# Mixing and routing the next block of tokens between the expert operations

## The reference, cut to what matters

```
g    = gelu(y_s5);  s5 = rmsnorm(g * sigmoid(g @ w_glu))      # w_glu 1024 x 1024
m2   = rmsnorm of (y * silu(z)), by halves of 512
x    = x + concat(s5, m2) @ w_out                             # w_out 2048 x 1024
h    = rmsnorm(x);  q = h @ w_q                               # w_q 1024 x 2048: 8 heads x 2 halves x 128
s    = q . sub_keys                                           # 16 key rows of 128 scores per token
top 16 of each key row -> 16 x 16 sums per head -> top 16 of those: 8 x 16 = 128 experts, gate = softmax
x    = x + sum over 128 experts of gate * gelu(u[e] . h) * v[e]
y    = rmsnorm(x)
```

## Time and profile before

| what | us |
|---|---|
| median of 3 runs | 4684.44 (4682.33 to 4685.42) |
| the profiled execution's own time | 4684.25 |
| its span in the profile | 4682.5 |
| first transfer of `mix_out` | 1352.42 |
| first transfer of `route_and_experts` | 1792.81 |
| first gather | 1891.59 |

### The profile page before, as it was taken

How to read it: one execution, slowest core, us unless ns; L and a number is a source line. 1 busy time by engine, 2 the same in 40 slices (tenths; PEclk the granted TensorE clock), 3 DMA queues, 4 the chain that set the end, 5 groups by cost and what they waited for, 6 DMA issues and landing times.

```text
span 4682.5 us, 54327 instructions
## 1 busy us (share of the span) xinstructions
PE 2876.1 (61%) x17688; PEld 1481.5 (32%) x17688; DVE 2462.9 (53%) x4924; ACT 1290.2 (28%) x3117; POOL 1411.9 (30%) x1547
## 2 busy tenths in 40 slices
PE   8999590745559995554654744645645546447444
PEld 5766460723334444221311411411312213114110
DVE  1000529248831113576576675674675765766754
ACT  1110020112222321333333333333333333333332
POOL 3000320301100000444444444444443444444443
PEclk9999755866779997665755755756757658658555
DMA  4111300121131112899999999999999999999998
GB/s 163 52 50 36 75 2 2 43 101 30 39 160 66 46 54 97 349 421 420 415 421 400 421 421 405 420 420 404 420 419 400 421 419 405 421 407 420 421 415 362
DMA packets 258478, 1271.27 MB, mean 271 GB/s; under 512 B 63984, under 2 KB 98672, under 8 KB 118128
## 3 DMA queue, kind: packets, MB, share of 16 engines
q0 software_dynamic: 156672, 1140.92, 58.8%
q1 hardware_dynamic: 101536, 127.12, 8.2%
HBM read 1225.69 MB, written 40.09 MB: 270 GB/s over the span
## 4 chain that ended last, share of the span: by engine, by line
DMA 40%; issue 7%; PE 6%; ACT 4%; DVE 4%; POOL 1%; POOLq 0%; SPq 0%; DVEq 0%; ACTq 0%
DMA pe_ring<-in_uv,pe_index_now 39%; PE pe_acc L1858 3%; DVE pe_ring L1781 2%; PE pe_ps_q L1831 2%; ACT pe_mark L1629 1%; ACT pe_weight L1631 1%; PE pe_ps_t L1851 1%; ACT L1629 1%; DVE pe_work_a L1662 1%; POOL pe_ring L1570 1%; ACT L1620 1%; DMA pe_w_q<-in_w_q 0%; DVE pe_pos L1714 0%; DVE pe_work_b L1715 0%; PE pe_ps_s L1841 0%
## 5 line engine op out<-in xcount | busy, mean ns | idle before, releaser
L1781 DVE CUSTOM_DVE_ANT_0 pe_ring<-pe_ring,pe_h_rep 128x1024 f32<-128x1024 f32 x1088 | 1330.7, 1226 | 961.3 <-DMA pe_ring<-in_uv,pe_index_now 881.3
L1858 PE MATMUL pe_acc<-pe_ring,pe_weight 128*32 128x256 f32 x8704 | 1018.5, 560 | 1232.3 <-ACT pe_weight L1631 1203.4
L1570 POOL DMA_INDIRECT pe_ring<-in_uv,pe_index_now x1088 | 1198.0, 1101 | 1471.2 <-PE pe_acc L1858 1275.3
L1858 PEld LDWEIGHTS pe_acc<-pe_ring,pe_weight 128*32 128x32 f32 x8704 | 210.8, 131 | 1973.1 <-ACT pe_weight L1631 1863.6
L1629 ACT ACTIVATE pe_mark<-pe_eye,pe_dot 128x32 f32<-128x32 f32 x1088 | 349.4, 321 | 1744.1 <-DVE pe_dot L1781 1690.3
L1631 ACT ACTIVATE pe_weight<-pe_mark,pe_gate_now 128x32 f32<-128x32 f32 x1088 | 349.5, 321 | 35.1
L1831 PE MATMUL pe_ps_q<-pe_h_t,pe_w_q 128*128 128x128 f32 x2304 | 329.5, 303 | 1.9 <-DMA pe_w_q<-in_w_q 1.9
L1831 PEld LDWEIGHTS pe_ps_q<-pe_h_t,pe_w_q 128*128 128x128 f32 x2304 | 302.7, 213 | 60.1 <-issue 57.8
L372 PE MATMUL pj_bank<-pj_w_in,pj_normed_t 128*128 128x512 f32 (+1 forms) x720 | 267.6, 529 | 5.7 <-DMA pj_w_in<-in_w_in 5.7
L1392 PE MATMUL mo_ps_out<-mo_w_out,mo_both_t 128*128 128x512 f32 x576 | 251.1, 594 | 14.8 <-DVE mo_both_t L1342 11.9
L378 PE MATMUL pj_bank<-pj_normed_t,pj_w_in 128*128 128x128 f32 x1728 | 195.2, 275 | 0.0
(11 more groups left out here) (312 smaller groups left out, 3222.6 us busy)
## 6 DMA issues: line engine op xcount, KB each, us to landing
pe_ring<-in_uv,pe_index_now POOLq DMA_INDIRECT x1088
pe_w_q<-in_w_q SPq DMA_DIRECT2D x4, 2048.0 KB, 18.3
m2s_window<-scratch_xbc SPq DMA_DIRECT2D x8, 786.0 KB
pj_w_in<-in_w_in SPq DMA_DIRECT2D x1, 6144.0 KB, 39.5
scratch_xbc<-pj_chan_out SPq DMA_DIRECT2D x8, 768.0 KB, 5.1
pj_x<-in_x_all SPq DMA_DIRECT2D x9, 512.0 KB
scratch_u<-pj_token_out SPq DMA_DIRECT2D x9, 512.0 KB, 2.6
scratch_z<-pj_token_out SPq DMA_DIRECT2D x9, 512.0 KB, 3.7
```

The lines of the kernel that those rows point to most:

```text
L1570: nc.gpsimd.indirect_dma_start(out=ring[:, p, :], out_offset=None, in_=D["uv"], in_offset=bass.IndirectOffsetOnAxis(ap=row, axis=0)).then_ ...
L1781: V.tensor_tensor_reduce(out=ring[:, p, 0:D_MODEL], in0=ring[:, p, 0:D_MODEL], in1=h_rep[:, g % 2, :], scale=1.0, scalar=0.0, op0=ALU.mult ...
L1858: last = T.matmul(acc[j * PER:(j + 1) * PER, g % 2, 0:COLS], lhs(j), src[:, j * COLS:(j + 1) * COLS], start=first, stop=final)
```

## The change

`mix_out` is emptied, and its work becomes part of the last stage. The nine tiles are cut into four blocks, (0), (1, 2), (3, 4, 5), (6, 7, 8). For each block, mixing and routing are done for all its tiles together: matmuls of up to 384 columns with the weights as the standing operand. The weights are no longer held: for each block `w_glu`, `w_out` and `w_q` are loaded again in 20 pieces of 128 x 8 x 256 (rows of 1 KB, 1 MB in all) through three buffers `w_buf`. Block 0 is done ahead of the gathers; each other block is done between the expert operations of the block before it, by a list of steps with places, `after[n]`, that every engine's list follows. The router's selection is done in four units of four key rows and two heads, for all tiles of the block. All loops are written out. The ring has six slots in place of eight. POOL no longer copies the indices; ACT no longer copies x, h and gate (x is loaded a second time and h made again, on DVE).

The core of the diff:

```
-    RING = 8
-    OPS = SLOTS
+    RING = 6
+    WB = 3
...
+    BLOCK_OF = ((0,), (1, 2), (3, 4, 5), (6, 7, 8))
...
+    UNITS, UNIT = 4, 4
+    PIECES = 4 + 8 + PH
+    GLU, OUT, QUERY = 0, 4, 12
+
+    def block_steps(nb):
...
+        for i in range(nb):
+            t = 8 * i
+            add(t, "sp_y", i)
+            add(t, "sp_x0", i)
+            for dt, name in ((2, "act_g"), (3, "dve_gate"), (3, "pe_g"), (4, "act_gt"), (4, "act_sq"), (5, "dve_mn"), (6, "pe_m"), (7, "dve_mt")):
+                add(t + dt, name, i)
+        g0 = 8 * (nb - 1) + 6
+        done = {}
+        for c in range(KT):
+            for dt, name in ((0, "pe_glu"), (1, "act_sig"), (2, "dve_s5"), (3, "act_ss"), (4, "pe_ss")):
+                add(g0 + 2 * c + dt, name, c)
...
+        for q in range(4):
+            for half in range(2):
+                for i in range(nb):
+                    add(o0 + (2 * q + half) * nb + i, "pe_o", q, half, i)
...
+        for j in range(PAIR):
+            for dt, name in ((0, "pe_q"), (1, "act_q"), (2, "pe_s"), (3, "act_s")):
+                add(q0 + 3 * j + dt, name, j)
...
+        for u in range(UNITS):
+            k0 = q0 + 12 * u + 13
+            for n in range(16):
+                add(k0 + n, "dve_k", u, n)
+            add(k0 + 12, "act_e", u)
+        for s in range(PIECES):
+            add(0 if s < WB else done[s - WB], "sp_w", s)
...
+        s, room = FIRST[b - 1] * SLOTS, len(BLOCK_OF[b - 1]) * SLOTS - 26
+        split = int(0.42 * room)
+        for t, name, args in ev:
+            n = s + (t * split // q0 if t < q0 else split + (t - q0) * (room - split) // (last - q0))
+            after[n].append((name, (b,) + args))
...
+            def weights(b, s):
+                W = PIECES * b + s
+                if W >= WB:
+                    b0, s0 = divmod(W - WB, PIECES)
+                    if s0 < OUT:
+                        sp.wait_ge(glu_made, KT * b0 + 2 * s0 + 2)
...
+                sp.dma_start(w_buf[:, W % WB], rows).then_inc(w_in[W % WB], 16)
...
+                if n >= RING:
+                    pool.wait_ge(op_done, n - RING + 1)
+                    settle(pool, settled)
```

More of the change, by code:

```diff
@@ new lines, in route_and_experts @@
+    opening = []
+    after = [[] for n in range(NT)]
+    for b, tiles in enumerate(BLOCK_OF):
+        ev, q0, last = block_steps(len(tiles))
+        if b == 0:
+            opening += [(name, (b,) + args) for t, name, args in ev]
+            continue
+        s, room = FIRST[b - 1] * SLOTS, len(BLOCK_OF[b - 1]) * SLOTS - 26
[3 more added lines that the diff above has]
+            after[n].append((name, (b,) + args))
@@ L1445, in route_and_experts @@
+    uses = [(name, args) for steps in [opening] + after for name, args in steps if name in ("pe_g", "pe_m", "pe_h", "pe_c", "pe_rep")]
+    TURN = {use: n for n, use in enumerate(uses)}
     with ExitStack() as ctx:
@@ new lines, in _ @@
+            act.wait_ge(eps_set, 1)
+            for name, args in opening:
+                step(name, args)
+            for n in range(NT):
+                k, s = divmod(n, SLOTS)
+                p = n % RING
+                if s == 0:
+                    act.wait_ge(index_ready, k + 1)
+                act.wait_ge(dots_ready, n + 1)
+                A(mark[:, p, :], eye[:], ACT.Gelu_apprx_tanh, scale=dot[:, p:p + 1]).then_inc(mark_ready, 1)
+                act.wait_ge(mark_ready, n + 1)
+                A(weight[:, p, :], mark[:, p, :], ACT.Copy, scale=choice[:, k % 2, 1, s:s + 1]).then_inc(weight_ready, 1)
+                for name, args in after[n]:
+                    step(name, args)
@@ L1800, in _ @@
             V.tensor_copy(same[:], eye[:].unsqueeze(1).to_broadcast([P, GROUPS, PER])).then_inc(made, 1)
-            chain.start(0)
-            for g in range(ROUTE_STEPS):
-                route(0, g, False)
-            with dve.Fori(0, MAIN_TILES) as k:
-                tile(k, GROUPS, True)
-            tile(MAIN_TILES, SAMPLE // PER, False)
+            for name, args in opening:
+                step(name, args)
+            for n in range(NT):
+                G, p = n // PER, n % RING
+                if n % PER == 0:
+                    dve.wait_ge(taken, TURN["pe_rep", (G,)] + 1)
+                dve.wait_ge(rows_in[p], 16 * (n // RING + 1))
+                V.tensor_tensor_reduce(out=ring[:, p, 0:D_MODEL], in0=ring[:, p, 0:D_MODEL], in1=h_rep[:, G % 2, :],
+                                       scale=1.0, scalar=0.0, op0=ALU.mult, op1=ALU.add, accum_out=dot[:, p:p + 1]).then_inc(dots_ready, 1)
+                for name, args in after[n]:
+                    step(name, args)
         @block.tensor
@@ L1848, in repeat, with turn @@
[L1848 to L1855 removed]
+            def turn(use, src):
+                u = TURN[use]
+                if u:
+                    pe.wait_ge(taken, u)
+                for c in range(KT):
+                    last = T.transpose(ps_t[:, c, :], src[:, c * P:(c + 1) * P], ident[:])
+                last.then_inc(turned, 1)
```

1035 lines of the change are left out of this document (516 added, 519 removed).

## The result

The changed kernel takes 4722.96 us (median of 4 runs, 4720.95 to 4730.76), the kernel before 4684.22 beside it: a ratio of 1.0086, interval 1.0071 to 1.0101. It is slower by 0.86%, where 4650 and "faster" was forecast; the time lies within the range of 4560 to 4775, and on the other side of the kernel before. The profiled execution is the longest of the four, 4730.76 us.

The account below looks back on a forecast made before the run. It took the last stage as bound by the gathers' bytes, the earlier ones by PE and a one-tile chain. Opening 1529, DMA 2952, key selection 91, chains 60 and ends 16 gave 4648, stated as 4650; range 4560 to 4775.

Parts of the forecast that it names:

- first gather: Opening with block 0's work: the first gather goes out at about 1529 us instead of 1891.59, a gain of 362.
- 1088 gathers: Gather stage: every gather of 128 rows x 8 KB takes 2.485 us, 2704 us in all.
- pieces, loads, stores: DMA added within the gathers: 60 reloaded weight pieces 186 us, inputs, x and x_mid 62 us.
- key selection on DVE: Key steps within the gathers: DVE binds, adding 59 us in block 1, 32 in block 2, none in block 3; 91.
- chains through PE and ACT: Gated and output steps within the gathers: 11 us chains not all hidden by the ring, 20 us a block, 60 together.
- the 66 us at the loop ends: Eight loop ends of the old gather stage, where DVE waits for instructions: about 66 us lost, which unrolling removes.
- bound of 140: Upper end for the chain cost: 140 us if each of 24 gated steps loses the 5.8 us beyond the ring's margin.
- sign for "wrong": Gather stage: the prediction is wrong if DMA stays under 0.9 outside the key steps of blocks 1 and 2.
- weights late or chains longer: Slower outcome within the gathers, from late weight pieces or longer PE and ACT chains; chance 0.33.
- Weights late: Output products of blocks 1 to 3: pieces taking 23 us make PE wait and DMA idle; 4758 us, chance 0.33.
- POOL's starving: Key steps of blocks 1 and 2: DVE's denser work holds up POOL's gather issue; 5120 us, chance 0.02.
- all hidden: Gather stage: no chain cost of 60 us and weight pieces at 2.5 us each; 4554 us, chance 0.1.

Follow-up runs that it names:

- gathers alone: The changed kernel without mixing, routing and weights of blocks 1 to 3, all tiles using tile 0's experts and inputs: 4287.02 us, ratio 0.9149 to the kernel before.
- transfers alone: The changed kernel with blocks 1 to 3 reduced to their transfers beside the gathers, nothing computing on what they bring: 4510.46 us, ratio 0.9627 to the kernel before.
- no keys: The changed kernel without DVE's key selection for blocks 1 to 3, all tiles using tile 0's experts and gates: 4618.70 us, ratio 0.9859 to the kernel before.

## Why the prediction was wrong

The idea held: 367 us are gained ahead of the gathers (1891.6 to 1524.6; 362 forecast), and the work returns within them, but at some 400 us and not 330. The forecast gain was the small difference of two large sums, 34 us, and two terms were off by more than that, both to the slow side.

| term | forecast | measured | from |
|---|---|---|---|
| first gather | 1529 | 1525 | the trace after |
| 1088 gathers | 2704 | 2748 | gathers alone |
| pieces, loads, stores | 248 | 223 | transfers alone less gathers alone |
| key selection on DVE | 91 | 106 | no keys |
| chains through PE and ACT | 60 | 107 | the rest: 213 - 106 |
| ends | 16 | 14 | what is left of the gathers alone: 4287 - 1525 - 2748 |

The measured column adds to 4723. The fourth and fifth terms are split by leaving out one of them, and parts that overlap may be counted to either; the fifth is a remainder, with no run of its own. The second and third are not cut at quite the same place: the gathers alone load x a second time for every tile, some 10 us in all (an estimate: 8 x 0.52 MB at 420 GB/s), which the forecast has among its 248.

*The gathers' pace (44 us).* The step that failed is "Unrolling takes the 66 us at the loop ends away; my sum has that already, as it starts from 2.485". A gather without loops and beside nothing but its own tile's x and y takes 2.528. The 2.485 is the spacing of two dots with nothing else under way; in the gathers alone it is still the common one (median 2.49), but the mean is 2.528, with DMA busy throughout. The bytes of x and y are some 20 us of the 44 (an estimate: 8.9 MB at 420 GB/s); the rest was not traced to a cause. And most of the 66 was never lost at the loop ends. Before, the dots stop there for 11.4 us from start to start, and the next ones follow after some 1.15 each from the full ring. From the last dot of tile 0's loop to the sixth after it:

```profile
2219.60 1.23 DVE L1781 CUSTOM_DVE_ANT_0 pe_ring<-pe_ring,pe_h_rep 128x1024 f32<-128x1024 f32 x1 [1.26 <-DMA pe_ring<-in_uv,pe_index_now]
...
2237.85 1.23 DVE L1781 CUSTOM_DVE_ANT_0 pe_ring<-pe_ring,pe_h_rep 128x1024 f32<-128x1024 f32 x1 [1.02 <-DMA pe_ring<-in_uv,pe_index_now]
```

These six spacings take 18.3 us where six of 2.484 take 14.9: 3.4 lost, and about as much at each of seven ends (0.3 at the eighth). From the first dot to the last the gathers took 2775 us before and take 2748 alone without loops, so 27 of the 66 were gained; the other part was the pace itself, and the trace of the kernel before already held it.

*The chains (47 us).* "I take 20 for each block": without the keys' share, tile 0's stretch loses 96 - 40 = 56, that of tiles 1 and 2 80 - 42 = 38, that of tiles 3 to 5 only 5. I spread one price evenly, though block 1 has 42 gathers for its mixing and block 3 has 150. My line on the gated step names the gathers that should pass in it for blocks 2 and 3 (2.5 and 3.9) and leaves out block 1, where by the same list only 1.4 do: 3.5 us of transfers for steps that follow each other after 7.2. The bound of 140 that I named was the better guide for a short stretch: there the chain isn't a loss on top of DMA, it is the pace, and the transfers under it are free (72 us given back by leaving out 186 us of pieces).

*The keys.* 106 for 91, but 40, 42 and 32 by blocks, not 59, 32 and 0. The forecast compared sums of busy time with sums of transfer time; lumps of more than the ring's margin cost time where the sums say hidden. Where I had DVE bind it did: it is busy for 156.9 of 165.4 us in block 1's key steps (1774.60 to 1940.00).

*The signs and the rivals.* The sign for "wrong" came as named: DMA stands at 0.84 over block 1's first 42 gathers, where no key step lies. The 0.33 was for "weights late or chains longer", and the second half came, for which no rival had a price. "Weights late" was on the right side, for the wrong reason: pieces are slow to land (medians of 18 to 43 us), but SP runs far enough ahead. PE waits for a piece 10.6 us in the whole run:

```profile
PE pe_bg L1879 <- DMA pe_w_buf<-in_w_out: 10.6, 3, 9.4
```

(total us, times, longest). With two buffers and 1 KB rows a part of that rival does appear (43.7 us). The rule of the Trainium skill, "DMA: Bandwidth & Descriptors", section Queues, rings and completion order, that each engine goes round its queue rows packet by packet, and by which alone 23 us a piece would hold, is borne out in so far as 23 lies among the medians of 17.7, 26.6 and 42.8; it says nothing of who waits for the pieces. Neither POOL's starving (an issue takes 1.13 us on the mean beside the steps, 0.97 in the last 320 gathers) nor "all hidden" occurred.

## What to carry to other kernels

Work moved under a bound resource cost, at each place of this kernel, about the longest of transfers, busiest engine and the chain through all of them (the chain in block 1's mixing, the transfers in block 3's), not their sum and not a mean price; so work out the chain for the shortest stretch first, and lay the steps over every operation there is, without two long ones side by side. When a forecast is the difference of two sums of some 350 us, take the pace of the largest term from whole tiles of the trace, loads and stores included, and not from its best stretches. A run with the transfers alone and one with the main stream alone split such a sum directly.
